# Latent attention without stages of its own: normalising on features, rotating and transposing heads inside the up-projections

## The reference, cut to what matters

```python
def mla_mixer(u, pos, w_in, q_norm_g, w_q_up, kv_norm_g, w_kv_up, w_out):
    c_q, c_kv, k_rope = jnp.split(u @ w_in, [384, 640], axis=-1)          # 672 columns
    q = (rms_norm(c_q, q_norm_g) @ w_q_up).reshape(bsz, seq, 16, 64 + 32)
    kv = (rms_norm(c_kv, kv_norm_g) @ w_kv_up).reshape(bsz, seq, 16, 64 + 64)
    q = jnp.concatenate([q[..., :64], rope(q[..., 64:], pos)], axis=-1)
    k_rope = jnp.broadcast_to(rope(k_rope[:, :, None, :], pos), (bsz, seq, 16, 32))
    k = jnp.concatenate([kv[..., :64], k_rope], axis=-1)
    out = chunk_causal_attention(q, k, kv[..., 64:], pos, 96 ** -0.5)
    return out @ w_out
```

## Time and profile before

| | us |
|---|---|
| median of 3 runs | 1659.3 |
| the profiled execution's own time | 1656.16 |
| its span, first to last instruction | 1654.2 |
| latent attention, input projection's first matmul to attention's first | 907.2 to 996.4 |

### The profile page before, as it was taken

One profiled execution on the slowest core, in us unless ns is written; L12 is line 12 of the kernel. 1 busy time (PEld: TensorE's weight loads), 2 busy tenths in 40 slices (PEclk: granted clock), 3 DMA queues, 4 the chain that ended last, 5 costly groups with the idle time before them and its releaser, 6 DMA issues. The chain is left out here.

```text
span 1654.2 us, 23359 instructions
## 1 busy us (share of the span) xinstructions
PE 1472.4 (89%) x8783; PEld 1260.6 (76%) x8783; DVE 1158.5 (70%) x2080; ACT 870.7 (53%) x1606; POOL 0.2 (0%) x4
## 2 busy tenths in 40 slices
PE   3999999996979999999998568899997997799887
PEld 2888879886858888788887565688886994599745
DVE  5988878868659888788888455786677345454364
ACT  1554454552446445564544447655555965485463
POOL 0000000000000000000000000000000000000000
PEclk9999999998979999999999789999998998799987
DMA  9899768530036897578784160395556440546000
GB/s 368 316 327 330 278 208 270 175 115 1 1 102 229 299 338 242 177 270 327 280 297 142 42 241 1 105 313 189 185 162 214 154 171 1 153 125 195 40 1 26
DMA packets 197515, 306.46 MB, mean 185 GB/s; under 512 B 10562, under 2 KB 159132, under 8 KB 197404
## 3 DMA queue, kind: packets, MB, share of 16 engines
q1 hardware_dynamic: 195744, 303.55, 53.9%
q10 hardware_dynamic: 1660, 1.43, 0.3%
HBM read 303.91 MB, written 1.05 MB: 184 GB/s over the span
## 5 line engine op out<-in xcount | busy, mean ns | idle before, releaser
L926 PE MATMUL bank<-u_hi_lo,w_hi 128*128 128x512 f32 x1344 | 473.8, 397 | 12.2 <-DVE arena L988 12.2
L925 PE MATMUL bank<-u_hi_lo,w_lo 128*128 128x256 f32 x1176 | 328.6, 279 | 0.0
L977 DVE TENSOR_TENSOR w_lo<-weight_ring,w_hi 128x1024 fp32r<-128x1024 f32 x264 | 307.8, 1220 | 12.0 <-ACT w_hi L947 11.3
L926 PEld LDWEIGHTS bank<-u_hi_lo,w_hi 128*128 128x128 f32 x1344 | 246.8, 188 | 63.7 <-DVE arena L988 15.1
L947 ACT CAST w_hi<-weight_ring 128x1024 fp32r<-128x1024 f32 x264 | 260.3, 1047 | 11.2 <-DMA weight_ring<-in_ffn_w_up_dram 5.5
L925 PEld LDWEIGHTS bank<-u_hi_lo,w_lo 128*128 128x128 f32 x1176 | 222.5, 189 | 7.4
L1197 DVE TENSOR_TENSOR wp_lo<-weight_ring,wp_hi 128x1024 fp32r<-128x1024 f32 (+4 forms) x149 | 167.7, 1164 | 59.1 <-ACT wp_hi L1164 58.8
L848 PE MATMUL bank<-src_hi,wp_hi 128*128 128x256 f32 (+1 forms) x632 | 183.1, 300 | 0.5 <-ACT src_hi L434 0.3
L1164 ACT CAST wp_hi<-weight_ring 128x1024 fp32r<-128x1024 f32 (+4 forms) x149 | 143.8, 1008 | 62.8 <-PE bank L848 56.5
L848 PE MATMUL bank<-src_lo,wp_hi 128*128 128x256 f32 (+1 forms) x632 | 173.6, 286 | 0.0
L848 PE MATMUL bank<-src_hi,wp_lo 128*128 128x256 f32 (+1 forms) x632 | 173.5, 286 | 0.0
(11 more groups left out here) (358 smaller groups left out, 2209.4 us busy)
## 6 DMA issues: line engine op xcount, KB each, us to landing
weight_ring<-in_mod_w_dram SPq DMA_DIRECT2D x72, 1024.0 KB, 6.9
weight_ring<-in_ffn_w_gate_dram SPq DMA_DIRECT2D x44, 1024.0 KB, 6.0
weight_ring<-in_ffn_w_up_dram SPq DMA_DIRECT2D x44, 1024.0 KB, 5.5
weight_ring<-in_ffn_w_down_dram SPq DMA_DIRECT2D x44, 1024.0 KB, 8.3
weight_ring<-in_hyb_w_in_dram SPq DMA_DIRECT2D x16, 1024.0 KB, 8.2
weight_ring<-in_w_in_e_dram SPq DMA_DIRECT2D x16, 1024.0 KB, 5.5
weight_ring<-in_w_in_o_dram SPq DMA_DIRECT2D x13, 1024.0 KB, 5.7
weight_ring<-in_hyb_w_out_dram SPq DMA_DIRECT2D x4, 1024.0 KB, 4.8
```

The lines of the kernel that those rows point to most:

```text
L925: nc.tensor.matmul(bank[:, 0:SEQ], w[1], u[:, 0:SEQ], start=False, stop=False, skip_group_check=True)
L926: last = nc.tensor.matmul(bank[:, :], w[0], u, start=kt == 0, stop=kt == KT - 1, skip_group_check=True)
L977: nc.vector.tensor_tensor(part_view(wl, n, part), raw, part_view(wh, n, part).bitcast(F32), ALU.subtract).then_inc(w_lo.sem, w_lo.up())
```

## The change

The three jobs of the input projection now put the first 640 columns on features (features on partitions, tokens along the row), which needs no transposes. ScalarE squares each bank while it takes it out. TensorE sums the squares over the partitions by a product with a matrix of ones, as the tail of the stage; ScalarE makes Ln and Exp of the sums, VectorE multiplies by root and gain, whose columns now come with the parameter rows at the start (two more small loads, 105 columns for 100; two broadcast loads of rows are gone). The 32 columns of the keys' rotary part keep tokens on partitions and share the third job. Angles, mask and sines are done by VectorE and ScalarE within this stage.

In the up-projections the keys' rotary part is rotated in VectorE's round 2, the queries in rounds 5 and 8 in two halves; the 16 groups of 4 transposes go ahead of jobs 7 to 13 on TensorE (one group or two each) and five behind the last job. ScalarE copies the query groups out, VectorE the key groups. The scaling of the queries is given to attention's own scale. There are 4 weight slots for 5. The scaling of x by LayerNorm rows moves to the output projection (rounds 2 and 3 of its 4 jobs), and so does its tile in the ring. Compressed rows lie in `uT`, the values in `zT`. `row_norms`, `bank_jobs`, `transposes` and three helpers go.

```diff
-        bc_w = {"qn": 384, "kvn": 256, "lam": 256, "a_log": 4, "dt_bias": 4}
+        bc_w = {"lam": 256, "a_log": 4, "dt_bias": 4}
...
+                    (2, 100, D["mla_q_norm_g"].rearrange("b (r d) -> (b r) d", d=P)),
+                    (2, 103, D["mla_kv_norm_g"].rearrange("b (r d) -> (b r) d", d=P))]
...
-        ROWS_C = 100
+        ROWS_C = 105
...
-                        head=None, x_rows_of=None, dve_at={}, tail=None):
...
-            wh, wl = (t[:, :].rearrange("p (s n) -> p s n", s=slots) for t in halves(room, "wp", slots * KT * P))
...
+                        head=None, x_rows_of=None, dve_at={}, tail=None, piece=KT * P):
...
+            wh, wl = (t[:, :].rearrange("p (s n) -> p s n", s=slots) for t in halves(room, "wp", slots * piece))
...
+            projections([job(t) for t in range(KT // 2)], src, held, tok=tok, tail=tail,
+                        x_rows_of=x_rows_of)
...
+        def log_exp_tables():
+            nc.scalar.preload_act_table_set("natural_log_exp_and_others")
...
+            room = uT.rearrange("p k t -> p (k t)")
+            cT = room[:, 0:5 * SEQ].rearrange("p (k t) -> p k t", k=5)
+            temps = [room[:, 5 * SEQ + 256 * i:5 * SEQ + 256 * (i + 1)].rearrange("p (a h n) -> p a h n", a=TT, h=8)
+                     for i in range(3)]
+            vtok = zT.rearrange("p k t -> p (k t)").rearrange("p (a n) -> p a n", a=TT)
+            kr = arena.take(TT * 32, "p (a n) -> p a n", a=TT)
...
-            row_norms([(cin[:, :, 0:384], bc["qn"], 1.0, cin[:, :, 0:384]),
-                       (cin[:, :, 384:640], bc["kvn"], 1.0, cin[:, :, 384:640])])
-            jobs = [transposes([cin[:, a, c * P:(c + 1) * P] for c in range(4)], cT[:, 0:4, a * P:(a + 1) * P])
-                    for a in range(TT)]
-            jobs.append(transposes([cin[:, a, 4 * P:5 * P] for a in range(TT)],
-                                   cT[:, 4, :].rearrange("p (a t) -> p a t", a=TT)))
-            bank_jobs(jobs)
...
+            def sines(act):
+                act.wait_ge(angles_ready.sem, angles_ready.base + 1)
+                nc.scalar.activation(rope_cs, ang, ACT.Sin)
+                log_exp_tables()
+            def latent_job(t):
+                tile, k, k0, fill, _ = proj_T(w_in, 256 * t, 256, None)
+                def take(copy, bank):
+                    b = bank[:, :].rearrange("p (k t) -> p k t", k=2)
+                    nc.scalar.activation(sq[:, 2 * t:2 * t + 2, :], b, ACT.Square)
+                    return copy(cT[:, 2 * t:2 * t + 2, :], b)
+                return tile, k, k0, fill, take
+            def last_fill(bank, wt, kt, src, term=None):
+                product(bank[:, 0:SEQ], (wt[0][:, 0:P], wt[1][:, 0:P]), src, kt == 0, kt == KT - 1, group=True)
+                return fill_tok(32, KT, P, SEQ, 32, False)(bank, wt, kt, src)
+            def last_take(copy, bank):
+                nc.scalar.activation(sq[:, 4, :], bank[:, 0:SEQ], ACT.Square)
+                copy(cT[:, 4, :], bank[:, 0:SEQ])
+                return copy(kr, bank[:, SEQ:SEQ + TT * 32].rearrange("p (a n) -> p a n", a=TT))
+            def latent_sums(pe, *_):
+                for i, (ka, kb) in enumerate(latents):
+                    pe.wait_ge(job_taken.sem, job_taken.base + 2 + i)
+                    for k in range(ka, kb):
+                        last = nc.tensor.matmul(PB[4 + i][:, 0:SEQ], ones[:, :], sq[:, k, :], start=k == ka,
+                                                stop=k == kb - 1)
+                    last.then_inc(latent_sum.sem, latent_sum.up())
+            def latent_roots(act):
+                for i, (ka, kb) in enumerate(latents):
+                    act.wait_ge(latent_sum.sem, latent_sum.base + i + 1)
+                    nc.scalar.activation(r[:, i, :], PB[4 + i][:, 0:SEQ], ACT.Ln, bias=eps[:, 1:2],
+                                         scale=1.0 / (P * (kb - ka))).then_inc(sstep.sem, sstep.up())
+                    act.wait_ge(sstep.sem, sstep.count)
+                    nc.scalar.activation(r[:, i, :], r[:, i, :], ACT.Exp, scale=-0.5) \
+                        .then_inc(latent_root.sem, latent_root.up())
+            def latent_scales(dve):
+                for i, (ka, kb) in enumerate(latents):
+                    dve.wait_ge(latent_root.sem, latent_root.base + i + 1)
+                    for k in range(ka, kb):
+                        nc.vector.scalar_tensor_tensor(out=cT[:, k, :], in0=cT[:, k, :],
+                                                       scalar=colT[:, 2 * P + 100 + k:2 * P + 101 + k], in1=r[:, i, :],
+                                                       op0=ALU.mult, op1=ALU.mult)
+            jobs = [latent_job(t) for t in range(2)]
+            jobs.append((lambda: cols_tile(w_in, 512, 160), KT, 0, last_fill, last_take))
+            def angles_and_visible(dve):
+                angles(dve)
+                visible(dve)
+            projections(jobs, uT, held, head=head, act_post={1: sines, 2: latent_roots}, dve_at={2: angles_and_visible},
+                        post={2: latent_scales}, tail=latent_sums)
...
+                    copy(kv4[:, :, 2 * t:2 * t + 2, 0:64], b[:, :, :, 0:64])
+                    return copy(v4[:, :, 2 * t:2 * t + 2, :], b[:, :, :, 64:128])
...
-            projections(jobs, cT, slots=5, x_rows_of=(3, 10))
...
-                nc.vector.tensor_scalar(qtok, qtok, scale, None, ALU.mult).then_inc(step_done.sem, step_done.up())
...
-            bank_jobs(jobs)
...
+            def turn_by(dve, x1, x2, n, t):
+                cos = rope_cs[:, :, 0:16].unsqueeze(2).to_broadcast([P, TT, n, 16])
+                sin = rope_cs[:, :, 16:32].unsqueeze(2).to_broadcast([P, TT, n, 16])
+                t1, t2, t3 = (v[:, :, 0:n, :] for v in t)
+                nc.vector.tensor_tensor(t1, x1, cos, ALU.mult)
+                nc.vector.tensor_tensor(t2, x2, sin, ALU.mult)
+                nc.vector.tensor_tensor(t3, x1, sin, ALU.mult).then_inc(vstep.sem, vstep.up())
+                dve.wait_ge(vstep.sem, vstep.count)
+                nc.vector.tensor_tensor(x1, t1, t2, ALU.subtract).then_inc(vstep.sem, vstep.up())
+                dve.wait_ge(vstep.sem, vstep.count)
+                nc.vector.tensor_tensor(t1, x2, cos, ALU.mult).then_inc(vstep.sem, vstep.up())
+                dve.wait_ge(vstep.sem, vstep.count)
+                return nc.vector.tensor_tensor(x2, t1, t3, ALU.add)
+            def turn_keys(dve):
+                x = kr.unsqueeze(2)
+                turn_by(dve, x[:, :, :, 0:16], x[:, :, :, 16:32], 1, temps).then_inc(vstep.sem, vstep.up())
+                dve.wait_ge(vstep.sem, vstep.count)
+                nc.vector.tensor_copy(kv4[:, :, :, 64:96], kr.unsqueeze(2).to_broadcast([P, TT, 16, 32])) \
+                    .then_inc(keys_turned.sem, keys_turned.up())
+            def turn_queries(dve, i):
+                if i:
+                    dve.wait_ge(queries_turned.sem, queries_turned.base + i)
+                x = q4[:, :, 8 * i:8 * i + 8, :]
+                turn_by(dve, x[:, :, :, 64:80], x[:, :, :, 80:96], 8, temps) \
+                    .then_inc(queries_turned.sem, queries_turned.up())
+            order = {7: [("q", 0)], 8: [("q", 1)], 9: [("q", 2), ("k", 0)], 10: [("q", 3), ("k", 1)], 11: [("k", 2)],
+                     12: [("q", 4), ("k", 3)], 13: [("q", 5), ("k", 4)],
+                     14: [("q", 6), ("k", 5), ("q", 7), ("k", 6), ("k", 7)]}
+            groups = [g for j in sorted(order) for g in order[j]]
+            copied = {"q": queries_copied, "k": keys_copied}
+            def heads_bank(i):
+                return PB[4 + i % 4]
+            def features(pe, j):
+                for which, g in order[j]:
+                    i = groups.index((which, g))
+                    if which == "q":
+                        pe.wait_ge(queries_turned.sem, queries_turned.base + 1 + g // 4)
+                        src = q4
+                    else:
+                        pe.wait_ge(keys_turned.sem, keys_turned.base + 1)
+                        pe.wait_ge(job_taken.sem, job_taken.base + 7 + g)
+                        src = kv4
+                    if i >= 4:
+                        w, n = groups[i - 4]
+                        pe.wait_ge(copied[w].sem, copied[w].base + n + 1)
+                    for n in range(2):
+                        for a in range(TT):
+                            o = (TT * n + a) * P
+                            last = nc.tensor.transpose(heads_bank(i)[0:96, o:o + P], src[:, a, 2 * g + n, :], ident)
+                    last.then_inc(heads_turned.sem, heads_turned.up())
+            def copy_group(eng, copy, which, g):
+                i = groups.index((which, g))
+                eng.wait_ge(heads_turned.sem, heads_turned.base + i + 1)
+                dst = (qT if which == "q" else kTt)[0:96, 2 * g:2 * g + 2, :]
+                copy(dst, heads_bank(i)[0:96, :].rearrange("p (h t) -> p h t", h=2)) \
```

(16 more changed lines are left out.)

218 lines of the change are left out of this document (39 added, 179 removed).

## The result

| | before | after |
|---|---|---|
| median, us (lowest to highest) | 1659.68 (1658.55 to 1662.34, 4 runs) | 1632.33 (1632.15 to 1634.81, 4 runs) |
| the profiled execution | 1656.16 | 1632.25 |
| its span | 1654.2 | 1630.4 |

The ratio is 0.984, with a 95% interval of 0.9822 to 0.9857: 27 us faster. Predicted were 1633 and a range of 1626 to 1643.

What follows compares the result with a forecast made beforehand. TensorE's matmuls bound most of the span, so time is gained only where TensorE idles or runs slowly. 9.0 + 17.0 = 26.0 us off 1656.16 gives 1630.2; with the median 3.1 above, 1633 us, range 1626 to 1643.

Steps and rivals of the forecast that it cites:

- Part 1: Input projection's third job: 48 narrow matmuls at 0.11 make it 8.2 us for 5.2, 3.0 us lost.
- rival of cheap narrow matmuls: Third job: the 48 narrow matmuls take 0.7 to 1.2 us rather than 5.3, total 1629; chance 0.13.
- The burst that the prediction leaned on: Trace of the kernel before: 8 matmuls with 2 columns, 0.95 us together, at most 0.12 each, against cheap narrow matmuls.
- Part 2: Input projection's end to up-projections' first matmul: 19.0 us becomes 7.0; 9.0 gained after Part 1's loss; sums 0.48 each.
- rival of reloaded tables: Latent sums' chain: Ln and Exp each load a table again, three loads of 1.28 us, total 1637; chance 0.05.
- Parts 3 and 4: Up-projections with 44 transposes, 31.8 us, and tail to attention, 3.1: 51.9 becomes 34.9, 17.0 us gained.
- The two pauses of 2.5 us go with the scaling of x: Up-projections: moving VectorE's scaling of x out removes TensorE's two pauses, 29.5 us becoming 27.0 before transposes are added.
- the rotations' 2.6 us: Up-projections, rounds 5 and 8: VectorE's rotations delay the queued low-half split by 2.6 us, covered by three jobs.
- The rival of stalls: Up-projections: copies and rotations queued with the splits stall TensorE, 5 us or 5.2 more, total 1638 to 1643; chance 0.12.
- the one of a clock that stays at half: Up-projections stay at clock 0.50, costing 23.7 us, total 1657, or 1675 if it lasts into attention; chance 0.03.
- Part 5: Output projection, ring and start: the moved scaling of x, 4.9 us of VectorE, and the moved loads cost nothing.
- The sum: Whole kernel: 9.0 + 17.0 = 26.0 us gained, 1630.2 for the profiled execution, median 3.1 above it, 1633 us.

Runs made afterwards that it cites:

- wide_rope: Changed kernel with the 32 rotary columns on features too: 24 matmuls of 256 columns for 48 of 32; 1627.3 us, ratio 0.9797 to the kernel before.
- rows_back: Changed kernel with the scaling of x by LayerNorm rows back in the up-projections, out of the output projection; 1633.8 us, ratio 0.9848 to the kernel before.
- turns_last: Changed kernel with all 16 groups of head transposes behind the last up-projection job, none between jobs; 1632.8 us, ratio 0.9842 to the kernel before.
- back_only: Kernel before with only the changed up-projections and tail, keeping its old input projection, row norms and transposes; 1643.1 us, ratio 0.9891 to the kernel before.
- fill3: wide_rope with three filler matmuls, results unused, in the input projection's tail behind the sums; 1631.1 us.

## Why the prediction was right

The time, the sign and the mechanism were right, and all five parts can be read in the profile; but one price was right by luck, and two of the reasons do not hold. In the order of the prediction:

- **Part 1** was right. From the first of six narrow matmuls to the second it is 0.03, from each other one to the next 0.11 to 0.12, and the 256-column matmul behind them takes 0.20 for 0.12 (921.03 to 921.23). So a feature tile takes 1.03 us (its first product is at 921.03 and the next tile's at 922.06), of which 0.67 are the narrow form's, and eight take 8.2. The weight loads of the six start 0.11 apart, and the first of them lies under a 256-column matmul. wide_rope confirms it from the other side. The rival of cheap narrow matmuls falls. The burst that the prediction leaned on, 8 records with 2 columns, is 4 matmuls in the code; each record has a weight load of its own, so its 0.12 stands as the price of one load. The Trainium skill's page TensorE: Matmul & The Clock Gate, in its section on LDWEIGHTS, prices a weight load by its columns, which for 128 makes about 107 ns. The trace agrees, with 0.11. The floor near 25 ns stands in that page's section Back-to-back issue gap for matmuls without the time of their weight loads, and the section itself says that it counts too little where each has one. So it did not speak for cheap narrow matmuls as the prediction has it, and it appears here only in the 0.03 of the first.
- **Part 2** was mis-sized in one execution by one term. The up-projections begin at 936.88 for 935.5, and 7.6 us are gained for 9.0. The term is the sums: priced at 5 x 0.48 = 2.4, they took 4.0, at a granted clock of 0.60. In rows_back and turns_last the same sums took 2.40, and rows_back's "in to up" is 28.15, which is 37.26 - 28.15 = 9.1 gained. So the chain as a whole was priced rightly at full clock, and what the prediction left out is that this stretch too can be at half clock. The price of 0.48 itself was luck. It came from 3.8 us over 8 records, but in the code these are 4 matmuls, each of which leaves two records, and that stretch of the kernel before was at a granted clock of 0.50:

```profile
1407.40:1411.20 3.80, 3.77 (x8) 2.49 (x8) 0.00 (x0) 1.14 (x2) 0.00 (x0) 0.50 1.02 319
```

That is 0.95 for a matmul at half clock, and the two misreadings cancel against the 0.46 to 0.48 at full clock. The rival of reloaded tables falls, by ScalarE's rows.
- **Parts 3 and 4**: 51.9 to 34.8, 17.1 gained for 17.0. The up-projections with their 44 transposes took 31.4 us from first to last start, for 31.8, and the tail 3.3 for 3.1. Inside, two reasons were wrong. "The two pauses of 2.5 us go with the scaling of x": by rows_back 2.1 of them would have gone with the transposes between the jobs. And the rotations' 2.6 us were said to be covered by three jobs, but the second one begins while TensorE is in job 7, and the low half queued behind it is job 9's: by turns_last 0.7 us of it shows where no transposes stand between the jobs. The rival of stalls falls, since TensorE has no wait above 0.5 us inside the stage, with 0.95 us of slack at job 9; so does the one of a clock that stays at half, which was at 0.50 for 4.9 us and at 1.00 from there.
- **Part 5** was right: rows_back undoes the move and the output projection comes out the same, 19.05 us from its first matmul to VectorE's first work on its banks, for 18.91 in after. Before it was 18.28, with a granted clock of 0.57 over the first 4 us and 1.00 over the next 5, for 0.50 and 0.91 after: 0.6 us given back by the clock and not by the move; back_only, which has the move too, needs 18.27.
- **The sum**: the offset is 24.8 at attention's first matmul, for 26.0, and 23.8 at the end of the span. The prediction then added 3.1 us for the distance of the median from the profiled execution. After's median is 0.1 above its profiled execution. A miss of 2.1 us (23.9 between the profiled executions for 26.0) and one of 3.0 nearly cancelled, so the closeness of 0.7 us is partly luck, as is the price of the sums.

## What to carry to other kernels

Where a fast engine waits through chains of small work, look first for stages that can be merged: both halves gained by that (7.7 and 17.5 us alone), and where in the merged stage the work stood mattered by about 1 us, mostly because transposes between the jobs covered a rotation of 2.4 us in VectorE's queue. A matmul that streams few columns behind a full weight load costs the load; swapping operands so that the few columns are the weights saved 2.4 us. Read an edit of 2 us in its own stretch of the trace and not in the total, and when a new work item is placed in a stage's tail, ask whether the next stage's start waits for it. Before a row's mean is used as the price of one instruction, compare its count with the code and look up the clock of its stretch.

## What was not expected of the hardware

- One stage can have a granted clock of 0.60 or of 1.00 with the same code and the same work ahead of it: the sums took 3.98 us in two executions and 2.40 in two. Unedited stages differed by up to 11 us in the profiled executions (615.6 to 626.5), with a granted clock of 0.61 to 0.83 over the last full 50 us; the same kernel, wide_rope, had 615.6 and 618.6.
- An idle stretch of 2.5 us ahead of the up-projections still left them 1 us at full clock before the fall (fill3), one of 4.5 us none.
- A matmul in full fp32 leaves two records: five of 128x256 show as x10 in 2.32 us at 1.00, which is 0.46 each, while one of fp32r takes 0.12.
- A transpose of 128 x 96 takes 7.15 / 64 = 0.112 us with its copies keeping up, whether in a block or two groups at a time (0.79 for 8).
